# Two projections around a cross attention moved from plain float32 matmuls to three passes over high and low parts, with the weight stores behind them given out later

## The reference, cut to what matters

```python
def memory_attention(h, mem_n, w_cq, w_ckv, w_co):
    q = (h @ w_cq).reshape(B, S, MEM_HEADS, MEM_DH)          # 1024 -> 512
    k, v = jnp.split((mem_n @ w_ckv).reshape(B, M, 2, MEM_HEADS, MEM_DH), 2, axis=2)
    s = jnp.einsum('bqhd,bkhd->bhqk', q, k) * (MEM_DH ** -0.5)
    p = jax.nn.softmax(s, axis=-1)
    o = jnp.einsum('bhqk,bkhd->bqhd', p, v).reshape(B, S, MEM_W)
    return o @ w_co                                          # 512 -> 1024

x = x + mixer(rmsnorm(x, g_mix), ...)
x = x + memory_attention(rmsnorm(x, g_cross), mem_n, w_cq, w_ckv, w_co)
x = x + hier_moe(rmsnorm(x, g_moe), ...)                     # every token goes to 2 of 32 experts
```

## Time and profile before

| | us |
|---|---|
| median of three executions | 1620.82 |
| the profiled execution, its own time | 1622.88 |
| the profiled execution, its span | 1621.1 |
| PE busy in the span | 1449.0 |
| DVE busy | 763.2 |
| ACT busy | 578.3 |
| bytes moved | 374.56 MB, a mean of 231 GB/s |

### The profile page before, as it was taken

How to read it: one execution, slowest core, us unless ns; L and a number is a source line. 1 busy time by engine, 2 the same in 40 slices (tenths; PEclk the granted TensorE clock), 3 DMA queues, 4 the chain that set the end, 5 groups by cost and what they waited for, 6 DMA issues and landing times.

```text
span 1621.1 us, 23932 instructions
## 1 busy us (share of the span) xinstructions
PE 1449.0 (89%) x10631; PEld 1206.0 (74%) x10631; DVE 763.2 (47%) x1088; ACT 578.3 (36%) x708; POOL 2.9 (0%) x8
## 2 busy tenths in 40 slices
PE   7998999899767777677899899999999988999998
PEld 5696899755433434333888799999988878999997
DVE  2546564421101101101786676666367757765642
ACT  2452552221100100000546655434243665544431
POOL 0000000000000000000000000000000000000000
PEclk9997999999988988889999999999999999999999
DMA  6553147499999999999534335556534323546540
GB/s 206 208 187 120 53 156 314 185 406 426 427 427 426 427 427 427 425 427 416 180 131 150 111 107 177 185 169 221 192 121 141 119 105 117 195 156 204 188 155 27
DMA packets 116272, 374.56 MB, mean 231 GB/s; under 512 B 7767, under 2 KB 53127, under 8 KB 103623
## 3 DMA queue, kind: packets, MB, share of 16 engines
q1 hardware_dynamic: 112199, 370.70, 59.6%
q0 software_dynamic: 528, 2.04, 0.4%
q10 hardware_dynamic: 3440, 0.25, 0.2%
HBM read 371.92 MB, written 1.06 MB: 230 GB/s over the span
## 4 chain that ended last, share of the span: by engine, by line
PE 66%; DMA 18%; DVE 10%; ACT 4%; issue 1%; ACTq 1%; SPq 1%; DVEq 0%
PE bank L605 33%; DMA ring<-in_w_exp_up 10%; PE bank L1161 7%; PE bank L629 4%; DVE parts L1640 3%; PE bank L979 3%; DMA tail_hn<-in_w_exp_up 3%; DMA SZ<-in_w_exp_up 3%; PE bank L827 2%; DMA ring<-in_w_in 2%; PE bank L949 2%; PE bank L1006 2%; PE bank L583 2%; PE bank L651 2%; ACT parts L1255 1%
## 5 line engine op out<-in xcount | busy, mean ns | idle before, releaser
L605 PE MATMUL bank<-hnr,parts 128*128 128x256 f32 x4032 | 500.0, 286 | 7.6 <-DVE Gr L1792 6.8
L605 PEld LDWEIGHTS bank<-hnr,parts 128*128 128x128 f32 x4032 | 492.9, 194 | 13.4 <-DVE Gr L1792 7.2
L1640 DVE TENSOR_TENSOR parts<-ring,parts 128x2048 fp32r<-128x2048 f32 x148 | 333.7, 2288 | 129.4 <-ACT parts L1255 127.9
L1255 ACT ACTIVATE parts<-ring 128x2048 fp32r<-128x2048 f32 x146 | 271.5, 1902 | 105.5 <-PE bank L1161 58.7
L979 PE MATMUL bank<-ring,TMP 128*32 128x512 f32 x608 | 88.9, 734 | 47.9 <-DMA ring<-in_w_exp_up 47.2
L605 PE MATMUL bank<-SKr,parts 128*128 128x256 f32 x960 | 119.9, 288 | 8.6 <-DVE SKr L2031 5.8
L605 PEld LDWEIGHTS bank<-SKr,parts 128*128 128x128 f32 x960 | 118.6, 196 | 9.2 <-issue 9.1
L1161 PE MATMUL bank<-Gr,parts 128*128 128x256 f32 x640 | 115.3, 283 | 0.0
L1986 DVE COPY KV<-bank 128x256 f32<-128x256 f32 x16 | 6.8, 425 | 219.7 <-PE bank L966 219.7
L979 PEld LDWEIGHTS bank<-ring,TMP 128*32 128x32 f32 x608 | 23.5, 130 | 105.4 <-issue 90.2
L1161 PEld LDWEIGHTS bank<-Gr,parts 128*128 128x128 f32 x640 | 99.9, 192 | 0.0
(11 more groups left out here) (324 smaller groups left out, 1637.4 us busy)
## 6 DMA issues: line engine op xcount, KB each, us to landing
ring<-in_w_in SPq DMA_DIRECT2D x60, 1024.0 KB, 7.3
ring<-in_w_ffn_in SPq DMA_DIRECT2D x44, 1024.0 KB, 7.3
ring<-in_w_exp_gate SPq DMA_DIRECT2D x19, 2048.0 KB, 39.7
ring<-in_w_exp_up SPq DMA_DIRECT2D x19, 2048.0 KB, 44.2
ring<-in_w_exp_down SPq DMA_DIRECT2D x18, 2048.0 KB, 39.3
ring<-in_w_ffn_out SPq DMA_DIRECT2D x20, 1024.0 KB, 6.1
G<-in_w_exp_gate SPq DMA_DIRECT2D x7, 2048.0 KB, 38.6
tail_hn<-in_w_exp_up SPq DMA_DIRECT2D x7, 2048.0 KB, 43.1
```

The lines of the kernel that those rows point to most:

```text
L605: m = mm(b(name)[:, T * half:T * half + T], part(chunk, ws)[:, k, P * mt:P * mt + P], src[xs][:, k, :], start=k == 0 and i == 0, stop=k == ...
L1255: A(parts[:, 2 * (r % 2), 2048 * i:2048 * i + 2048], ring[:, CHUNK[chunk][0], 2048 * i:2048 * i + 2048], ACT.Copy).then_inc(high_made, 1)
L1640: v.tensor_tensor(parts[:, 2 * (r % 2) + 1, at], ring[:, CHUNK[chunk][0], at], parts[:, 2 * (r % 2), at].bitcast(F32), ALU.subtract).then_ ...
```

## The change

cq and co join SPLIT and are taken in three passes. The normed input of cq and the attention's output are split in high parts (ACT) and low parts (DVE) as they are made, in Gr; the plain copy of co0 to co3 by DVE becomes a copy by ACT (high) and a subtraction by DVE (low). The parts of cq lie in ring 2 and 3, those of co in ring 4 and 5, so these stores come free later. The stores 0 and 2 change places, and the first fills are given out in a new order.

```diff
-SPLIT = [n for n in ALL_CHUNKS if not n.startswith(("ckv", "cq", "co"))]
+SPLIT = [n for n in ALL_CHUNKS if not n.startswith("ckv")]
-        stores = ((ring[:, 4], ring[:, 5]), (G[:, 2048:6144], tail_hn[:, :]), (hx[:, :], SZ[:, :]), (ring[:, 0], ring[:, 1]),
+        stores = ((hx[:, :], SZ[:, :]), (G[:, 2048:6144], tail_hn[:, :]), (ring[:, 4], ring[:, 5]), (ring[:, 0], ring[:, 1]),
                   (ring[:, 2], ring[:, 3]))
-        qc, oc = view(G, 0, 4, T), view(G, 1024, 4, T)
+        qc = view(G, 0, 4, T)
+        cross_parts = (view(Gr, 2048, KT, T), view(Gr, 4096, KT, T))
+        oc_parts = (view(Gr, 1024, 4, T), view(Gr, 0, 4, T))
...
-            used(sp, "out0")
-            fill(1, 1, 4, store_landed[4])
             used(sp, "out1")
             fill(0, 0, 0, store_landed[0])
-            fill(0, 2, 2, store_landed[2])
+            used(sp, "cq")
+            fill(1, 1, 4, store_landed[4])
             full(sp, "co3")
             fill(0, 1, 1, store_landed[1], slots=(0,))
-            used(sp, "cq")
             used(sp, "co")
+            fill(0, 2, 2, store_landed[2])
             fill(1, 0, 3, store_landed[3])
...
-            linear_f("cq", hn, ["cq0", "cq1"], h_at=16)
+            split_f("cq", cross_parts, ["cq0", "cq1"], (cross_split, 0))
...
-                        m = mm(b(name)[:, T * half:T * half + T], w[:, k, P * (2 * j + half):P * (2 * j + half) + P],
-                               oc[:, k, :], start=k == 0, stop=k == 3)
+                        ready("co", k, 4)
+                        for i, (ws, xs) in enumerate(PASSES):
+                            m = mm(b(name)[:, T * half:T * half + T], part("co", ws)[:, k, P * (2 * j + half):P * (2 * j + half) + P],
+                                   oc_parts[xs][:, k, :], start=k == 0 and i == 0, stop=k == 3 and i == 2)
...
+            def cross_beside(j):
+                act.wait_ge(h_ready, 8 * NORMS.index("n_cross") + 2 * j + 2)
+                A(two(cross_parts[0], j), two(hn, j), ACT.Copy).then_inc(cross_high, 1)
+                if j == 1:
+                    high("cq")
+            def take_oc(h):
+                full(act, f"co{h}")
+                A(oc_parts[0][:, h, :], b(f"co{h}")[:, 0:T], ACT.Copy).then_inc(oc_high, 1)
-            norm_squares("n_cross", xres, [f"ou{j}" for j in range(4)])
+            norm_squares("n_cross", xres, [f"ou{j}" for j in range(4)], cross_beside)
             norm_root("n_cross")
+            high("co")
...
                 if h < 3:
                     cross_exp(h + 1)
                 take(f"ct{h}", cprobT[h % 2])
+                if h:
+                    take_oc(h - 1)
+            take_oc(3)
...
                     if not x:
                         gain_apply("g_cross", 0, j)
+                        if j:
+                            cross_low(j - 1)
+                        if j == 1:
+                            low("cq")
...
+            cross_low(3)
             link(v.reciprocal(root, root))
+            low("co", [0])
             take_scaled("cq0", two(qc, 0), over_tiles(root))
+            low("co", [1])
             take_scaled("cq1", two(qc, 1), over_tiles(root))
...
-                freed(v.tensor_copy(oc[:, h, :], b(f"co{h}")[:, 0:T]), f"co{h}")
+                dve.wait_ge(oc_high, h + 1)
+                freed(v.tensor_tensor(oc_parts[1][:, h, :], b(f"co{h}")[:, 0:T], oc_parts[0][:, h, :].bitcast(F32), ALU.subtract), f"co{h}")
```

More of the change, by code:

```diff
@@ L275, in part @@
             name = chunk.split(".")[0]
-            k = 4 if name.startswith(("down", "proj")) else 8
+            k = 4 if name.startswith(("down", "proj", "co")) else 8
             return parts[:, 2 * (SPLIT.index(chunk) % 2) + which, :].rearrange("p (k n) -> p k n", k=k)
@@ L376, in build @@
             "route_diff", "route_exp", "mask_ready", "keys_ready", "count_ready"))
+        cross_high, cross_split, oc_high = sem("cross_high"), sem("cross_split"), sem("cross_out_high")
         sq_summed, tok_root_ready, masks_made = sem("sq_summed"), sem("tok_root_ready"), sem("masks_made")
@@ L877, in _ @@
                 emptied(pe, f"co{h}")
-            landed(pe, "co")
-            w = tall[CHUNK["co"][0]]
             def route_logits(ks):
@@ L1825, in z_low, with cross_low @@
                 v.tensor_tensor(two(z_parts[1], j), two(z1, j), two(z_parts[0], j).bitcast(F32), ALU.subtract).then_inc(z_split, 1)
+            def cross_low(j):
+                dve.wait_ge(cross_high, j + 1)
+                v.tensor_tensor(two(cross_parts[1], j), two(hn, j), two(cross_parts[0], j).bitcast(F32), ALU.subtract).then_inc(cross_split, 1)
             def merge(x, n):
```

## The result

| | kernel before | changed kernel |
|---|---|---|
| median, six executions of each | 1621.07 us | 1628.86 us (1623.8 to 1630.95) |
| ratio, with its 95% interval | | 1.0045 (1.003 to 1.006) |
| profiled execution: its own time, its span | 1622.88, 1621.1 us | 1629.33, 1626.4 us |

By the ratio, the change makes the kernel slower by 0.45%, 7.3 us (4.9 to 9.7); the two medians lie 7.8 us apart. The forecast was + 4.4 us, in a range of + 1.2 to + 8.0 (1622.0 to 1628.8 us). The size forecast was 3 us too small: both differences lie at the upper end of the range, past the + 7 us that the likely case was given, and the median as a time, 1628.86 us, is 0.06 us above the upper bound. All ratios here are of fast executions, which leaves out one later execution of each kernel (3502 and 3976 us).

The account below looks back on a forecast made before the run. The DMA queue was taken as the bound from about 341 us to the experts' end. Two late transfers + 9.8, earlier co - 3.5, vanished dry spell - 1.95 gave + 4.4 us: median 1625.2 us, range 1622.0 to 1628.8.

Parts of the forecast that it names:

- the likely case: The forecast outcome for the whole kernel: slower by 3.2 to 7 us, given a chance of 0.66.
- What bounds the kernel: From about 341 us to the experts' end the DMA queue is the bound, at 427 GB/s.
- The passes: cq and co on PE in three passes: 11.59 us for cq, 2.2 less, and 11.8 for co, 2.4 less.
- Their cover: Making the weights' parts on ACT and DVE costs nothing; third residual sum slips 2.7 us; 2.3 us if cover is gone.
- The heads: In the four heads before co, ACT's copy and DVE's step cost 1.1 us more, bounds 0.4 and 2.9.
- The stores: Before co is full, five expert transfers go out, not seven; four go out together at 316.0 us.
- + 9.8: Two expert transfers, 4.194 MB, move from idle time into the full queue: 9.8 us more at 427 GB/s.
- 1.95: The queue's dry spell from 338 to 342 us vanishes, 0.83 MB: 1.95 us less.
- The signs named beforehand: Trace signs: groups of about 11.6 us, issue times, no rate under 400 GB/s from 320 to 350, next layer about 782.6.
- one sign of being wrong: The queue empty anywhere between 330 and 740 us would show the prediction wrong.
- PE's wait for the second expert of pair 0: PE waits until about 344.8 us at no cost; a pair costs PE 21 us, the queue 29.5.
- The page's figure: A limit of about 358 GB/s from HBM per core; the prediction said the trace, at 427, doesn't agree.

Follow-up runs that it names:

- Pair 1's group last: The changed kernel with the fill of pair 1's first group put behind the last transfer of pair 0; ratios 1.0037 and 1.0029 to the kernel before.
- the order alone: The kernel before with only the new stores and new order of fills, cq and co in plain float32; ratio 1.0042.

## Why the prediction was right, and what it missed

*What bounds the kernel.* Right. The distance to the next layer followed the count of late transfers: one late + 2.8, two late + 8.8, two late with an earlier co + 4.8 where the queue stayed full, none late with an earlier co - 4.6 us. The chain of the kernel before, which reads PE up to 396 us, would have made all of these equal or the change faster.

*The passes.* cq took 11.51 us (forecast 11.59, before 13.81). co took, from its first matmul to its last, 13.5 us where it had 15.84, 2.3 less (forecast 2.4).

*Their cover.* Right: DVE's third residual sum slipped and the fourth didn't, against the earlier trace rows:

```profile
268.17 0.68 DVE L1623 TENSOR_TENSOR xres<-bank,xres 128x512 f32<-128x512 f32 x1
...
271.43 0.69 DVE L1623 TENSOR_TENSOR xres<-bank,xres 128x512 f32<-128x512 f32 x1 [1.33 <-PE bank L607]
```

*The heads.* Forecast + 1.1 us, measured + 0.55. The order on ACT was as foreseen, to be read against the earlier trace rows:

```profile
294.54 1.55 PE L869 MATMUL bank<-G,KV 128*128 128x256 f32 x4
...
296.12 0.38 ACT L1384 ACTIVATE Gr<-bank 128x256 fp32r<-128x256 f32 x1 [0.79 <-PE bank L869]
296.40 0.47 ACT L1395 ACTIVATE G<-bank,sm 128x256 f32<-128x256 f32 x1
...
301.33 0.42 DVE L1908 TENSOR_TENSOR Gr<-bank,Gr 128x256 fp32r<-128x256 f32 x1 [0.53 <-ACT Gr L1384]
```

The exponential of head 3 does wait behind the copy of co0. But the product of head 0 met less of the low clock and took 1.55 us, not 1.92, so that it ended 9.7 us behind cq and not 10.5, and the 14.4 us from cq's end to the last product stayed 14.4. What is left is the copy ahead of DVE's subtraction: PE starts co 1.30 us behind the last product, and 0.77 before. In all co is full 4.1 us earlier behind out1 (44.2 for 48.4 us; 3.7 on the mean of two and four traces); forecast 3.5.

*The stores.* Right in count and place. + 9.8 - 4.1 - 1.95 would be + 3.8; the two executions with a full queue show + 4.8. From co's issue on they need 8.3 us more than the kernel before, where 9.8 - 1.95 is 7.9, for the new queue still lost a little (334 and 367 GB/s from 338 to 342 us). The rest is that co came earlier by 3.5 us in these two, against the mean of the two traces before, and not by 4.1.

*The signs named beforehand.* The two groups, SP's issues and the heads came as said. Two signs of being right did not: the rate fell under 400 GB/s between 320 and 350 us (382 from 338 to 342), and the next layer's first matmul stood at 785.08, not at about 782.6. And one sign of being wrong did appear, in two of four traces: the queue ran short between 330 and 740 us.

*The step that failed* is the sentence on PE's wait for the second expert of pair 0: "That costs nothing: a group is still in the queue whenever PE frees a store". The wait itself was foreseen, to 344.8 us; it ended at 346.9. What I left out is what a wait of 12 us does to PE. In the trace the granted clock falls to 0.50 during it, and the 32 matmuls behind take up to 6.59 us in place of 3.64. The second group comes free 5 us later than reckoned. The queue then held one group, 9.8 us of work, which was too little: dry spells of (427 - 344) x 4 + (427 - 317) x 6 = 0.99 MB, 2.3 us. From co's issue to the landing the two traces with dry spells need 2.5 and 2.9 us more than the other two. The second and larger of the two spells has a second cause, the slow product with the down weights (5.08 us), and the trace that lacks it shows hardly any (399 GB/s from 364 to 370 us); how much of the 2.3 us belongs to the late expert alone is not shown. I had checked the margin with a pair's mean time (21 us against 29.5) and not for this first pair, where only one group stood in the queue. Pair 1's group last takes the wait away and with it 0.0007 of the ratio in one series, which is not clear of noise, and 0.0028 in the other, which is. The four distances average + 6.0 us, while the three series of the changed kernel gave + 7.1 to + 9.2. The 1 to 3 us between them stay open: four traced executions need not stand for all, and the distances leave out both ends of the kernel. So the sum was right to half a microsecond where the queue stayed full; that the measured time fell inside a range that has no term for dry spells was in part luck.

*The page's figure.* The rate of the full queue was 426 or 427 GB/s in every trace from 370 to 740 us, so the 358 GB/s of the Trainium skill (DMA: Bandwidth & Descriptors, Specifications) did not hold for this program, which runs on one core alone. The + 5.9 us worked out from it came nearer the result than + 4.4 by chance.

## What to carry to other kernels

When a DMA queue is full for good from some moment on, count the transfers that are done by then; an edit that speeds up engines ahead of it pays only by the time at which the last buffer comes free, and one that holds a buffer until the queue is full costs the whole transfer. To compare versions that differ by less than their executions do, measure between two events of the trace that enclose the edit as closely as possible: here the last such stretch repeated within 0.2 us over six traces, where whole times differ by microseconds. Look at the chain beside the rate: a chain that reads PE up to the first long transfer can still be bound by the queue. When parts are made of loaded data, the loaded copy is free at once, so give its place to the next load before anything else.

## What the runs showed of the hardware that I had not expected

A wait of PE for a landing, 9.5 to 12.2 us in four executions of the same program, costs more than itself: the granted clock fell to 0.50 (1.2 GHz) within it, and the next 32 matmuls took 4.92, 4.98, 6.14 and 6.59 us, where without the wait they take 3.64. How long the low level lasted once PE worked again differed from execution to execution. With 4.92 and 4.98 us, and 5.54 in the order alone, the queue of weights, a few us deep at that point, stayed full behind it; with 6.14 and 6.59 it ran dry. Later pairs have such slow groups too, in both kernels (5.34 us at 557.01 in the changed kernel's first trace), and the rate stays at 427 GB/s: there the queue is deep enough.
